# First attention of a two-block kernel: another order of head sums, low parts and exchanges

## The chip, the cores and the metric

The kernel runs on one core of one Trainium2 chip. The time is the device time of one execution in microseconds; the median of several executions is compared. The engines are TensorE (PE in the rows; PEld is its weight load), VectorE (DVE), ScalarE (ACT), GpSimd (POOL) and SyncE (SP). ACTq is ScalarE's queue where it issues DMAs.

## The reference, cut to what matters

Two models run one after the other on 256 tokens of width 1024: a recurrent layer, a feed-forward, an attention layer, a feed-forward, and then two layers of a second block. The change is in the attention layer:

```python
def attention_layer(x, norm_g, w_qkv, q_norm, k_norm, w_out):
    b, l, _ = x.shape
    h = rmsnorm(x, norm_g)
    qkv = (h @ w_qkv).reshape(b, l, 3, ATT_HEADS, ATT_HEAD_DIM)
    pos = jnp.arange(l, dtype=jnp.float32)
    q = partial_rope(rmsnorm(qkv[:, :, 0], q_norm), pos) * (ATT_HEAD_DIM ** -0.5)
    k = partial_rope(rmsnorm(qkv[:, :, 1], k_norm), pos)
    v = qkv[:, :, 2]
    ...
```

There are 16 heads of 64. `rmsnorm` of q and k is taken over each head. `partial_rope` turns the first 16 of the 64 features of a head: the first 8 and the next 8 change places and are multiplied with the sine, all is multiplied with the cosine, and the two are added.

## The kernel before

Activations lie feature-major, 8 tiles of 128 features by 256 tokens. Every weight matrix comes in units: 1024 x 128 for queries and keys, half of the depth by 256 columns for values. The layer has 8 query units (`att_q`), 8 key units (`att_k`) and 8 value units (`att_v[0]`, `att_v[1]`, 4 each); the texts call them q0 to q7, k0 to k7 and v0 to v7. Products of float32 are made of three passes: a weight unit is split into a high part in rounded form and a low part, the rest. ScalarE writes the high part (L722, `high_act(through)`: all units up to that one that are still due), VectorE subtracts to get the low part (L733, `split_v(through)`), and TensorE multiplies high by high, high by low and low by high, 24 matmuls in a unit (L708, and L697 for the values).

There are 5 slots for raw units and 3 for high parts. SyncE loads unit u (L638) when unit u-5 is used; ScalarE can write the high part of unit u when unit u-3 is used. Two units make a half product of 512 columns in one of two banks; VectorE takes it to `Q` or `K` with the token scale (L2466, `scaled_halves_v`), ScalarE takes the value halves (L3424, `head_tokens_act`). `scaled_halves_v` with `more` 2 first writes the low parts up to two units past the half it then takes.

The token scale of the layer's norm is made by ScalarE, is turned by two transposes on TensorE behind q7 (L949), and ScalarE reads the turned form (`RSTD`, L3443), which is only needed for the values.

For the norm of the heads VectorE squares `Q` (L2459, into `SQA`) and later `K` (into `SQK`); TensorE sums them over each head with four products (L941, `head_sums_pe`), ScalarE takes four logarithms (L3411) and one exponential (L3416, together `head_scales_act`), and VectorE multiplies (L2474, `norm_heads_v`). Then comes the rotation: ScalarE issues four DMAs that change the places of the first 8 and next 8 features of each head (L3434, `swap_halves_act`, SBUF to SBUF, into `ROT`, which a memset at L2497 has cleared), VectorE multiplies with the cosine (L2479, `cos_v`), multiplies `ROT` with the sine when the exchange has landed (L2485) and adds (L2488); these last two are `rotate_v`. After the rotation of `K` VectorE releases `keys_ready`, for which TensorE waits before the heads (L1201, `attend_pairs_pe`). Seven value units stand before that wait, v7 between the first scores of the heads.

Each engine's instructions stand in the order in which the functions write them by hand; an engine that waits holds up all that stands behind. Semaphores are counted, and `due` gives the count that the next event will have.

## Time and profile before

| | us |
|---|---|
| median of three runs | 1932.09 |
| lowest, highest | 1929.77, 1934.56 |
| profiled execution | 1930.44 |
| its span | 1927.4 |
| gap before k0, and start of the heads | 2.65, at 492.67 |

Times in the rows are microseconds from the start of the span; durations of one instruction in nanoseconds are marked. A name behind an arrow in brackets is what released the engine from the idle time given. Views used are the page (shares of the chain that ended last), the chain in order of time, the timeline of single engines, busy times in given stretches with the granted clock of TensorE, and the landing times of one tensor's transfers. TensorE's float32 products of 512 columns stand in the timeline as two matmuls each, so four head sums are counted as eight.

### The profile page before, as it was taken

To read this page: it belongs to the slowest core of one execution; us is meant where nothing else is said; L and a number is where in the kernel's file an instruction comes from. 1 tells how busy PE (TensorE), PEld (TensorE's weight loads), DVE (VectorE), ACT (ScalarE), POOL (GpSimd) and SP (SyncE) were. 2 spreads that over 40 slices of the span, in tenths; PEclk is the share of its full clock that TensorE was granted. 3 is DMA by queue.
4 is the path that set the end of the run, shared out by engine and by line. 5 is a ranking of instruction groups with operands and counts; after the bars stand their busy time and mean duration, and the time that the engine had idled before them with its cause. 6 is when DMAs were issued, how large, how long until landed. Compare 5 with 4: busy or idle time off the path is not lost.

```text
span 1927.4 us, 42678 instructions
## 1 busy us (share of the span) xinstructions
PE 1849.3 (96%) x18447; PEld 1728.3 (90%) x18447; DVE 1339.1 (69%) x1723; ACT 814.6 (42%) x1219; POOL 88.3 (5%) x131
## 2 busy tenths in 40 slices
PE   8999999999899999999998999998999999999999
PEld 7987999998689999998987799897998997889988
DVE  8897688757748876764786469666774696459755
ACT  5573534435634342223755234254213664235154
POOL 2000000000400000002000000000002000000000
PEclk9999999999999999999999999999999999999999
DMA  8555477974337795663550145554563651135644
GB/s 224 144 144 152 129 264 257 271 201 137 105 99 250 264 267 136 164 174 94 163 153 15 47 119 165 145 146 128 145 185 88 163 154 47 28 105 160 172 118 134
DMA packets 473228, 291.94 MB, mean 151 GB/s; under 512 B 26775, under 2 KB 467580, under 8 KB 472872
## 3 DMA queue, kind: packets, MB, share of 16 engines
q1 hardware_dynamic: 466720, 262.13, 48.5%
q0 software_dynamic: 5312, 25.32, 3.5%
q10 hardware_dynamic: 1032, 2.11, 0.5%
q8 instruction: 126, 2.06, 0.5%
q14 instruction: 38, 0.31, 0.1%
HBM read 287.95 MB, written 1.05 MB: 150 GB/s over the span
## 4 chain that ended last, share of the span: by engine, by line
PE 79%; DVE 14%; ACT 4%; issue 2%; DMA 1%; ACTq 0%; POOL 0%; DVEq 0%
PE bank L708 37%; PE bank L1486 6%; PE bank L1488 6%; PE bank L1487 6%; DVE rounded L733 4%; PE bank L667 3%; PE bank L949 3%; PE bank L697 2%; ACT rounded L722 1%; PE bank L1692 1%; PE bank L1679 1%; PE bank L1116 1%; DVE rounded L717 1%; PE bank L790 1%; PE bank L941 1%
## 5 line engine op out<-in xcount | busy, mean ns | idle before, releaser
L708 PE MATMUL bank<-rounded 128*128 128x256 f32 x5928 | 719.1, 281 | 10.2 <-DVE rounded L733 7.9
L708 PEld LDWEIGHTS bank<-rounded 128*128 128x128 f32 x5928 | 700.8, 187 | 25.2 <-DVE rounded L733 12.3
L733 DVE TENSOR_TENSOR rounded<-arena,rounded 128x1024 fp32r<-128x1024 f32 (+1 forms) x307 | 370.6, 1215 | 102.5 <-ACT rounded L722 94.6
L1486 PE MATMUL bank<-parts 128*128 128x256 f32 x1024 | 287.2, 280 | 1.0 <-DVE parts L2323 0.9
L1488 PE MATMUL bank<-parts 128*128 128x256 f32 x1024 | 285.9, 279 | 0.0
L1487 PE MATMUL bank<-parts 128*128 128x256 f32 x1024 | 285.6, 279 | 0.0
L722 ACT ACTIVATE rounded<-arena 128x1024 fp32r<-128x1024 f32 x192 | 201.5, 1057 | 170.2 <-PE bank L708 103.5
L1486 PEld LDWEIGHTS bank<-parts 128*128 128x128 f32 x1024 | 192.8, 188 | 2.2 <-issue 1.2
L1488 PEld LDWEIGHTS bank<-parts 128*128 128x128 f32 x1024 | 192.3, 188 | 0.0
L1487 PEld LDWEIGHTS bank<-parts 128*128 128x128 f32 x1024 | 192.1, 188 | 0.1
L773 ACT ACTIVATE arena<-bank 128x512 f32<-128x512 f32 x90 | 53.2, 596 | 241.6 <-PE bank L708 227.7
L2395 ACT ACTIVATE parts<-whole 128x2048 fp32r<-128x2048 f32 x44 | 84.3, 1918 | 126.9 <-PE bank L1488 109.4
L717 DVE CAST rounded<-arena 128x1024 fp32r<-128x1024 f32 (+1 forms) x115 | 78.2, 680 | 69.2 <-PE bank L708 43.0
L2315 DVE TENSOR_TENSOR parts<-whole,parts 128x2048 fp32r<-128x2048 f32 x44 | 100.7, 2292 | 16.8 <-ACT parts L2395 16.1
L708 PE MATMUL bank<-arena 128*128 128x256 f32 x416 | 91.1, 379 | 0.0
L949 PE MATMUL bank<-common,arena 128*128 128x128 f32 x519 | 78.1, 285 | 13.3 <-DMA common<-in_const 7.1
L708 PEld LDWEIGHTS bank<-arena 128*128 128x128 f32 x416 | 78.9, 190 | 11.5 <-issue 1.0
L708 PE MATMUL bank<-common,arena 128*128 128x256 f32 x384 | 87.8, 383 | 0.0
L708 PEld LDWEIGHTS bank<-common,arena 128*128 128x128 f32 x384 | 71.2, 189 | 10.9 <-issue 0.3
L949 PEld LDWEIGHTS bank<-common,arena 128*128 128x128 f32 x519 | 58.6, 145 | 23.0 <-DMA common<-in_const 7.1
L2323 DVE TENSOR_TENSOR parts<-whole,parts 128x1408 fp32r<-128x1408 f32 x32 | 52.0, 1625 | 38.9 <-ACT parts L2427 38.8
L2427 ACT ACTIVATE parts<-whole 128x1408 fp32r<-128x1408 f32 x32 | 44.1, 1380 | 65.9 <-PE bank L1488 54.5
(407 smaller groups left out, 2405.8 us busy)
## 6 DMA issues: line engine op xcount, KB each, us to landing
arena<-in_w_in SPq DMA_DIRECT2D x190, 512.0 KB, 3.8
whole<-in_ffn_w_gate_up SPq DMA_DIRECT2D x44, 1024.0 KB, 5.2
arena<-in_ada_w POOLq DMA_DIRECT2D x32, 768.0 KB, 6.4
whole<-in_ffn_w_down SPq DMA_DIRECT2D x16, 1408.0 KB, 7.2
arena<-in_rec_w_in SPq DMA_DIRECT2D x36, 512.0 KB, 3.8
arena<-in_att_w_qkv SPq DMA_DIRECT2D x24, 512.0 KB, 3.8
arena<-in_rec_w_out SPq DMA_DIRECT2D x16, 512.0 KB, 3.7
arena<-in_mla_w_o SPq DMA_DIRECT2D x16, 512.0 KB, 3.7
```

Source lines behind the costliest of these rows:

```text
L667: last = pe.matmul(psum[s][:, i * T:i * T + T], w[a][:, kk, :], job.rhs[b][:, kk, :], start=(i, kk, a, b) == (0, 0, 0, 0), stop=kk == job. ...
L708: last = pe.matmul(psum[s][0:c, m % 2 * T:m % 2 * T + T], w[a][:, k, cols], x[b][:, k, :], start=(k, a, b) == (0, 0, 0), stop=k == job.kt ...
L717: write(high_view(job_of[u], u), raw_view(job_of[u], u, UNIT_RAW)).then_inc(done.sem, 1)
L722: high_parts(act, lambda to, frm: act.activation(to, frm, ACT.Copy), high_by_act[0].pop(0), unit_high_s)
L733: dve.tensor_tensor(raw_view(job_of[u], u, UNIT_LOW), raw, high_view(job_of[u], u).bitcast(F32), ALU.subtract)\
L773: return lambda i, bank, done, rounds: act.activation(two(dst, i, lo), bank, func).then_inc(done, 1)
L949: last = pe.transpose(bank[:, n * P:n * P + P], x, ident)
L1486: pe.matmul(bank, w_hi, x_hi, start=start and k == 0, stop=False)
L1487: pe.matmul(bank, w_hi, x_lo, start=False, stop=False)
L1488: last = pe.matmul(bank, w_lo, x_hi, start=False, stop=stop and k == n - 1)
L2315: dve.tensor_tensor(UP_W[s][1], WHOLE_UP[s], UP_W[s][0].bitcast(F32), ALU.subtract)\
L2395: act.activation(UP_W[s][0], WHOLE_UP[s], ACT.Copy)\
```

## The change

TensorE sums the squares of the query heads behind k1 in place of k3, and those of the key heads behind v0 in place of v1. ScalarE writes the high parts of k0 and k1 before it reads the turned scale, no longer writes a high part between logarithms and exponential, and issues the exchange of Q behind one high part (k5's) after the exponential; before, the exchange stood behind those of k7, v0, v1 and v2, too. The exchange of K stands behind v5's high part as before; the second logarithms come ahead of v4's high part. VectorE clears `ROT` before the last query half, takes key halves one at a time between the steps of Q's rotation, and the rotation is cut in two functions, so that low parts and a key half stand between the sine multiply and the addition.

```diff
@@ att_pe
-            multiply_units(att_k, range(4))
+            multiply_units(att_k, range(2))
             head_sums_pe(SQA, DK, abanks)
-            multiply_units(att_k, range(4, 8))
-            multiply_units(att_v[0], range(2))
+            multiply_units(att_k, range(2, 8))
+            multiply_units(att_v[0], range(1))
             head_sums_pe(SQK, DK, abanks)
-            multiply_units(att_v[0], range(2, 4))
-            multiply_units(att_v[1], range(2))
-            multiply_units(att_v[1], range(2, 3))
+            multiply_units(att_v[0], range(1, 4))
+            multiply_units(att_v[1], range(3))
@@ attention_v
-            scaled_halves_v(att_q, Q, 2, range(4))
+            scaled_halves_v(att_q, Q, 2, range(3))
             dve.memset(flat(ROT), 0.0)\
                .then_inc(vector_step.sem, 1)
             dve.wait_ge(vector_step.sem, vector_step.due(dve))
+            scaled_halves_v(att_q, Q, 2, range(3, 4))
             square_heads_v(Q, SQA)
-            scaled_halves_v(att_k, K, 2, range(2))
-            split_v(att_k.first + 6)
+            scaled_halves_v(att_k, K, 2, range(1))
+            split_v(att_k.first + 4)
             norm_heads_v(Q, "att_q_norm")
-            scaled_halves_v(att_k, K, 2, range(2, 4))
+            scaled_halves_v(att_k, K, 2, range(1, 2))
+            cos_v(Q)
+            scaled_halves_v(att_k, K, 2, range(2, 3))
+            sin_v()
+            scaled_halves_v(att_k, K, 2, range(3, 4))
             square_heads_v(K, SQK)
-            cos_v(Q)
-            split_v(att_v[0].first + 2)
-            rotate_v(Q)
+            rotated_v(Q)
+            split_v(att_v[0].first + 3)
+            norm_heads_v(K, "att_k_norm")
             split_v(att_v[1].first)
-            norm_heads_v(K, "att_k_norm")
-            split_v(att_v[1].first + 1)
             cos_v(K)
+            split_v(att_v[1].first + 2)
+            sin_v()
             split_v(att_v[1].through())
-            rotate_v(K)
+            rotated_v(K)
@@ att_act
-            high_act(att_q.through())
+            high_act(att_k.first + 1)
...
-            high_act(att_k.first + 2)
+            high_act(att_k.first + 4)
+            head_scales_act()
             high_act(att_k.first + 5)
-            head_scales_act(att_k.first + 6)
-            high_act(att_v[0].first + 2)
             swap_halves_act(Q)
+            high_act(att_v[0].first + 3)
+            head_scales_act()
+            high_act(att_v[1].first)
             head_tokens_act(0, range(1))
-            high_act(att_v[1].first)
-            head_scales_act()
             high_act(att_v[1].first + 1)
             swap_halves_act(K)
+            high_act(att_v[1].first + 2)
             head_tokens_act(0, range(1, 2))
             high_act(att_v[1].through())
```

ScalarE in the order of before, from the reading of the turned scale to the exchange of K. L3443 is that reading, L722 a high part (x6: k0 to k5), L3411 the logarithms, L3416 the exponential, L3434 an exchange, L3424 a value half.

```order
L3443 ACTIVATE common<-bank 128x2
L722 ACTIVATE rounded<-arena 128x1024 x6
L3411 ACTIVATE arena<-bank,common 128x512 x4
L722 ACTIVATE rounded<-arena 128x1024
L3416 ACTIVATE arena<-arena 128x2048
L722 ACTIVATE rounded<-arena 128x1024 x4
L3434 DMA arena<-arena 8x2048 x4
L3424 ACTIVATE arena<-bank,common 128x256 x2
```

The same stretch in the changed kernel, where the lines are L3447, L3417, L3420, L3438 and L3428.

```order
L722 ACTIVATE rounded<-arena 128x1024 x7
L3447 ACTIVATE common<-bank 128x2
L722 ACTIVATE rounded<-arena 128x1024 x3
L3417 ACTIVATE arena<-bank,common 128x512 x4
L3420 ACTIVATE arena<-arena 128x2048
L722 ACTIVATE rounded<-arena 128x1024
L3438 DMA arena<-arena 8x2048 x4
L722 ACTIVATE rounded<-arena 128x1024 x6
```

Two of the high parts have moved ahead of the reading (x7: q3 to q7, k0, k1), and five that stood between the first logarithms and the first exchange are one.

VectorE in the order of before, from the norm of Q to its rotation. L2474 is the norm, L733 a low part, L2466 a key half taken, L2459 the squares of K, L2479 the cosine, L2485 the sine, L2488 the addition.

```order
L2474 SCALAR_TENSOR_TENSOR arena<-arena,common 128x2048
L733 TENSOR_TENSOR rounded<-arena,rounded 128x1024
L2466 TENSOR_TENSOR arena<-bank,common 128x512
L733 TENSOR_TENSOR rounded<-arena,rounded 128x1024 x2
L2466 TENSOR_TENSOR arena<-bank,common 128x512
L2459 TENSOR_TENSOR arena<-arena 128x2048
L2479 TENSOR_TENSOR arena<-arena,common 128x2048
L733 TENSOR_TENSOR rounded<-arena,rounded 128x1024
L2485 TENSOR_TENSOR arena<-arena,common 128x2048
L2488 TENSOR_TENSOR arena<-arena 128x2048
```

The same stretch in the changed kernel; its lines are L2473, L2465, L2458, L2478, L2484 and L2489.

```order
L2473 SCALAR_TENSOR_TENSOR arena<-arena,common 128x2048
L733 TENSOR_TENSOR rounded<-arena,rounded 128x1024
L2465 TENSOR_TENSOR arena<-bank,common 128x512
L2478 TENSOR_TENSOR arena<-arena,common 128x2048
L733 TENSOR_TENSOR rounded<-arena,rounded 128x1024 x2
L2465 TENSOR_TENSOR arena<-bank,common 128x512
L2484 TENSOR_TENSOR arena<-arena,common 128x2048
L733 TENSOR_TENSOR rounded<-arena,rounded 128x1024 x2
L2465 TENSOR_TENSOR arena<-bank,common 128x512
L2458 TENSOR_TENSOR arena<-arena 128x2048
L2489 TENSOR_TENSOR arena<-arena 128x2048
```

Cosine and sine of Q have moved ahead of the last key half and of the key squares, and with the sine the wait for the exchange.

## Rows read from the trace of the kernel before

**Rows 1.** The page: shares of the chain that ended last, by engine.

```profile
PE 79%; DVE 14%; ACT 4%; issue 2%; DMA 1%; ACTq 0%; POOL 0%; DVEq 0%
```

**Rows 2.** The chain in order of time, 430 to 505: start us, us, engine, line.

```profile
434.85 2.36 DVE rounded L733 x2
...
438.37 1.78 DVE arena L2497
...
449.70 3.43 PE bank L941 x8
453.13 11.32 PE bank L708 x96
...
466.72 5.05 DMA arena<-arena
...
478.73 2.35 DVE arena L2474
...
483.09 0.64 ACTq L3434
...
485.67 2.36 DVE rounded L733 x2
...
490.27 2.30 DVE arena L2488
```

**Rows 3.** Timeline of TensorE: start, us, line; idle time before it and its releaser.

```profile
436.18 7.18 PE L708 MATMUL bank<-parts,rounded 128*128 128x256 f32 x48 [2.65 <-issue]
443.78 5.92 PE L708 MATMUL bank<-parts,rounded 128*128 128x256 f32 x48 [0.42 <-DVE rounded L733]
...
473.49 1.13 PE L941 MATMUL bank<-arena,common 128*128 128x512 f32 x2 [0.82 <-ACT arena L3411]
...
477.73 8.43 PE L697 MATMUL bank<-rounded,parts 128*128 128x256 f32 x72 [0.37 <-DVE rounded L733]
486.95 2.99 PE L697 MATMUL bank<-rounded,parts 128*128 128x256 f32 x24 [0.79 <-DVE rounded L733]
492.67 0.93 PE L1201 MATMUL bank<-arena 64*128 64x128 f32 x8 [2.73 <-DVEq L2515]
...
494.33 1.22 PE L1201 MATMUL bank<-arena 64*128 64x128 f32 x6 [0.73 <-DVE arena L1245]
...
495.91 5.13 PE L697 MATMUL bank<-rounded,parts 128*128 128x256 f32 x24
```

**Rows 4.** Busy times in three stretches; the last three columns are PEclk, DMA share, GB/s.

```profile
435.80:439.00 3.20, 2.82 (x13) 2.85 (x14) 2.64 (x4) 0.91 (x1) 0.00 (x0) 0.50 0.21 64
472.00:474.00 2.00, 1.18 (x3) 0.30 (x2) 2.00 (x1) 1.97 (x3) 0.00 (x0) 1.00 0.80 266
493.80:500.60 6.80, 6.27 (x30) 5.65 (x31) 5.38 (x15) 3.29 (x12) 3.83 (x6) 0.51 0.02 4
```

**Rows 5.** Timeline of ScalarE, columns as in rows 3.

```profile
424.92 1.06 ACT L722 ACTIVATE rounded<-arena 128x1024 fp32r<-128x1024 f32 x1 [1.76 <-PE bank L708]
433.56 0.17 ACT L3443 ACTIVATE common<-bank 128x2 f32<-128x2 f32 x1 [7.58 <-PE bank L949]
...
454.92 1.90 ACT L3416 ACTIVATE arena<-arena 128x2048 f32<-128x2048 f32 x1
...
464.56 2.79 ACTq L3434 DMA_DIRECT2D arena<-arena  x4
...
501.13 0.84 ACT L3424 ACTIVATE arena<-bank,common 128x256 f32<-128x256 f32 x2 [2.02 <-PE bank L697]
```

**Rows 6.** Timeline of VectorE, columns as in rows 3.

```profile
464.47 0.69 DVE L2466 TENSOR_TENSOR arena<-bank,common 128x512 f32<-128x512 f32 x1 [0.45 <-PE bank L708]
```

**Rows 7.** Busy times at the end of K's exchange, columns as in rows 4.

```profile
485.00:485.50 0.50, 0.50 (x7) 0.50 (x6) 0.00 (x0) 0.50 (x2) 0.00 (x0) 1.00 0.14 33
485.50:486.00 0.50, 0.50 (x6) 0.46 (x5) 0.33 (x1) 0.50 (x2) 0.00 (x0) 1.00 0.01 0
```

**Rows 8.** Tile view of the loads of in_att_w_qkv.

```profile
DMA to landing us min/median/max: 3.4/3.8/10.3
```

More of the change, by code:

```diff
@@ L2481, in cos_v, with sin_v @@
             dve.wait_ge(vector_step.sem, vector_step.due(dve))
-        def rotate_v(x):
+        def sin_v():
             dve.wait_ge(heads_swapped.sem, heads_swapped.due(dve, 64))
@@ L2487, in rotate_v, with rotated_v @@
             dve.wait_ge(vector_step.sem, vector_step.due(dve))
+        def rotated_v(x):
             dve.tensor_tensor(x, SQA, ROT, ALU.add)\
@@ L3405, in modulation_act, with head_scales_act @@
             act.nop().then_inc(modulation_summed.sem, 1)
-        def head_scales_act(through=None):
+        def head_scales_act():
             for k in range(0, DK, 2):
@@ L3413, in head_scales_act @@
                 act.wait_ge(free.sem, free.due(act))
-            if through is not None:
-                high_act(through)
             act.activation(flat(RS), flat(RS), ACT.Exp, scale=-0.5)\
```

## The prediction

> **What bounds the kernel now.** I read the page's chain first, then the chain, TensorE's timeline, the clock and the other engines' rows between 415 and 505 us, since the change touches nothing else. TensorE carries 79% of the chain, VectorE 14% [rows 1]: the kernel is a sequence of products with a few places where another engine is late. The first attention is such a place. I call its weight units q0 to q7, k0 to k7 and v0 to v7; each is 24 matmuls. Four of them take 11.32 us in the chain, so one takes 2.83 us, and the four sums of a head-sum group take 3.43 us [rows 2]. TensorE finishes the q units and the two transposes of the scale at 433.53 and begins the heads at 492.67. In between lie 15 units and two sum groups: 15 x 2.83 + 2 x 3.43 = 49.3 us. Fifty-nine pass, so 9.8 us are lost. Where: 2.65 us before k0, 0.42 before k2, 0.82 inside the second sums, 0.37 and 0.79 before value units, 2.73 before the heads [rows 3], in sum 7.8. The rest is clock: after the first gap 435.8 to 439 ran at 0.50 of full clock, which is the 1.2 GHz level [rows 4], and 48 matmuls took 7.18 us in place of 5.66 [rows 3], 1.5 us more. Together 9.3, and 0.5 of pipeline edges.
>
> What releases them: ScalarE reads the turned scale at 433.56 and only then makes the high parts of k0 to k2 [rows 5], so the k0 low part starts at 434.85 [rows 2] with TensorE empty. At the far end the heads wait for the rotated keys. Their chain is norm 478.73, exchange issued until 483.73, two late low parts at 485.67, rotation to 492.57 [rows 2].
>
> **Durations** on VectorE: a low part 1.18 us (two in 2.36, [rows 2]), taking a half product 0.69 [rows 6], the multiplies over the whole of Q or K 2.30 [rows 2]. On ScalarE a high part takes 1.06 [rows 5].
>
> **Part 1, two high parts ahead of the turned scale.** A high part starts 0.38 us after the unit three before it is done: q7's starts at 424.92 [rows 5], when q4 ended at about 424.5 (three units before the transposes begin at 433.1). k0's and k1's can so be at 427.7 and 430.6, in time in which ScalarE waits 7.58 us for the transposes [rows 5]. Removed: their 2 x 1.06 us behind 433.56. VectorE meets them with the memset (1.78 us, [rows 2]) moved ahead of the low parts: last-but-one q product taken by 428.4, memset 428.9 to 430.7, low k0 to 431.95, low k1 from 431.7 + latency to 433.15. k0 starts at 433.53 as the transposes end. The 2.65 us gap and the 1.5 us of slow clock behind it go: 4.2 us. The cover is VectorE's idle time there; if it is gone, the price is again the same gap.
>
> **Part 2, first head sums behind k1.** The q product is taken at 433.3 (0.33 after q7's end), squares 434.1 to 436.5 (2.30 us, [rows 2]). k0 and k1 run to 439.2, so the squares are ready, and the sums fill 439.2 to 442.65. The last logarithm ends 4.2 us after a sum group starts (449.70 to 454.92, less one high part between them, [rows 2, 5]), the exponential takes 1.90 [rows 5]: 445.4. VectorE's norm (2.35 us, [rows 2]) ends at 447.8. What is queued behind the waiting norm on VectorE is low k5, which TensorE needs at 451.2 and gets at 449.0. ScalarE now has k5's high part behind the logarithms, 445.8 to 446.9.
>
> **Part 3, exchange at the norm.** ScalarE issues the four DMAs at 447.8 in place of 464.56, in 2.79 us [rows 5], until 450.6. They stand ahead of the high parts of k6 and k7, which come 450.65 to 452.75. VectorE: takes k's second half by 449.7, cos to 452.1, low k6 and k7 to 454.5; TensorE wants them at 454.0 for k6 (ready 453.3) and 456.8. The exchange before landed 5.05 us after its last issue began, with weight loads beside it [rows 2]: here 450.0 + 5.05 = 455.05. VectorE is busy until 455.3 anyway (it takes k's third half first), so the price now is nil; each later microsecond is one of delay, because the sine multiply now stands ahead of low v0 and v1, the last k half and the key squares. Sine 455.3 to 457.6, low v0 and v1 to 460.0, take to 460.7, squares 460.85 to 463.15. TensorE finishes k7 at 459.6 and v0 at 462.45, so it waits 0.7 us here, a gap of the kind at 473.49, whose 0.82 us left the clock at 1.00 [rows 3, 4]. Sums 463.2 to 466.65; before, they ended after 474.
>
> **Part 4, the keys.** Logarithms to 467.45, exponential to 469.4, key norm 469.4 to 471.8, while VectorE first adds the rotated Q and splits v2 and v3 (463.2 to 467.9). ScalarE must make v5's high part first, which needs v2 done (472.3): 472.7 to 473.75. Exchange issue 473.8 to 476.55, v6's high part to 477.6. VectorE: low v4 to 473.0, cos to 475.35, low v5, low v6 to 478.85. Landing is the unknown. The earlier row gives 5.05 us behind the start of the last issue. The second exchange of the kernel before had no weight load beside it: last issue at 483.09, last traffic at about 485.5, and none after [rows 2, 7], so 2.4 us. After the change the last weight load of the stage (v7's) is issued when v2 ends and takes 3.8 us [rows 8], to about 476.2, while the last exchange issue starts at 475.85. I take the row without load, since only the first 0.35 us of the last transfer lie beside it: 478.3, hidden behind low v6. Ends: 478.3 and 480.9. Then sine 478.9 to 481.2, low v7 to 482.4, rotation to 484.7, heads at 484.8. TensorE ends v6 at 483.6 and waits 1.2 us. **492.67 - 484.8 = 7.9 us gained** (5.8 with the late landing).
>
> A rule speaks against my choice here. The Trainium skill, "DMA: Bandwidth & Descriptors", section "Issuing engines are not separate DMA queues", says that transfers run on the same 16 DMA engines and interleave whichever engine issued them. By it ScalarE's exchange would share its time with SyncE's load of v7 and land late, a gain of 5.8 in place of 7.9; it is the third case below, and the trace agrees with it as far as 5.05 us with loads and 2.4 without go.
>
> **After the keys** the instructions are unchanged and take their waits with them. One thing can differ. Before, the gap of 2.73 us was followed by 0.51 of full clock from 493.8 to 500.6 [rows 4], and v7 took 5.13 us in place of 2.83 [rows 3], with ScalarE waiting 2.02 us for it [rows 5]. If the clock stays at 2.4 GHz, v7 and two small score products end 3 us earlier, and 2.0 of them are worth something until ScalarE's wait is used up. The total idle time there falls from 2.73 + 0.73 to about 1.2 + 0.73 us, which lies between gaps that cost the clock (2.65, 2.73) and one that did not (0.82); I give the fall two chances in three.
>
> **Sum.** The profiled execution took 1930.44 us, of which 1927.4 are its span; 1930.44 - 7.9 = 1922.5. It lay 1.65 us under the median of 1932.09, so the median comes to 1924.2, a gain of 0.41%. Nothing behind the stage has a time of its own: weight loads wait on used units, the feed-forward on the heads.
>
> **The cases.**
> - Forecast, 0.44: keys at 484.8, clock falls again: 1924.2.
> - Clock holds, 0.22: 7.9 + 2.0 = 9.9 us, 1922.2. For it: less idle. Against: two idle pieces close together.
> - Second exchange lands late, 0.16: 5.8 us, 1926.3. For it: 5.05 in the row of the first exchange; v7's load is issued 1.2 us before the exchange and runs beside it. Against: three of its four transfers are small and the load is nearly over.
> - Both exchanges late, 0.11: 2 us more on the first shift everything behind the sine of Q, 3.9 us, 1928.2.
> - The gain is given back, 0.03: the change makes keys earlier but the heads wait for something else, 1932.1. Against: the timeline shows nothing but the keys at 492.67 [rows 3].
> - Slower, 0.04: the first exchange blocks VectorE. Before, 4.6 us of issue and landing lay behind the key squares, now they are ahead of them, so lateness reaches TensorE. The longest landing of a load in the trace is 10.3 us [rows 8]. With 10.3 in both exchanges: the first shifts by 10.3 - 5.05 = 5.2, the key exchange lands at 475.85 + 5.2 + 10.3 = 491.4, plus 5.9 of sine, low part and rotation gives 497.3, 4.6 us behind before: 1936.7. It decides against the change once the two delays add to 7.9 us.
>
> **How the numbers follow.** A measurement here tells about 0.3%, 5.8 us, from no change. The first two cases lie beyond it, the third just at it (half counts): 0.74 faster. Half the third, the fourth and fifth: 0.22 same. 0.04 slower. The range must hold the clock case (1922.2), the two late exchanges (1928.2) and the spread of the three runs, 2.4 us to either side: 1920 to 1929.
>
> **What would show it.** Right: k0 right behind the transposes with the clock at 1.00 through 433 to 445; the four exchange issues of Q near 448 and of K near 474; waits of about 0.7 us before the second sums and 1.2 before the heads. Wrong: a DMA wait ahead of either sine multiply, a TensorE wait at k6 (its low part has 0.7 us to spare), or heads at 487 and later.

## The result and the profile after

| | before | changed |
|---|---|---|
| median, us | 1930.99 | 1919.67 |
| lowest, highest | 1929.77, 1934.56 | 1916.98, 1922.08 |
| profiled execution | 1930.44 | 1922.08 |
| its span | 1927.4 | 1920.3 |

The medians lie 11.3 us apart; the ratio of changed to before, estimated from all executions of the comparison, is 0.9943, 95% interval 0.9931 to 0.9956. (So estimated, a ratio need not be the quotient of the two medians, here and below.) The forecast was 1924.2, 7.9 us less, and the range began at 1920.0, so the time is 0.33 us outside it, on the better side.

The chain of the changed kernel in order of time, 430 to 505 us (start, us, engine, line), which answers to [rows 2]:

```profile
436.31 5.66 PE bank L708 x48
441.97 3.45 PE bank L941 x8
...
448.17 2.36 DVE arena L2473
450.55 0.83 ACTq L3438
...
452.76 5.90 DMA arena<-arena
...
458.79 2.30 DVE arena L2484
...
464.18 2.30 DVE arena L2458
466.52 3.70 PE bank L941 x8
...
477.98 4.31 DMA arena<-arena
482.32 2.30 DVE arena L2484
...
485.87 2.21 DVE arena L2489
...
488.18 0.93 PE bank L1201 x7
```

Read it from the top. k0 and k1 take 5.66 us (L708, 48 matmuls) and the first head sums (L941) follow without a gap. The exchange of Q is issued as the norm ends, and now it is in the chain: norm, issue, landing, sine, squares, second sums. The same three kinds come again for K. In [rows 1] DMA had 1% of the chain; in the page of the changed kernel it has 2%:

```profile
PE 78%; DVE 13%; ACT 4%; issue 2%; DMA 2%; POOL 0%; ACTq 0%; DVEq 0%; SPq 0%
```

TensorE's timeline of the changed kernel (start, us, line, count, and in brackets the idle time before it and what ended it), which answers to [rows 3]:

```profile
436.07 5.90 PE L708 MATMUL bank<-parts,rounded 128*128 128x256 f32 x48
...
444.84 17.52 PE L708 MATMUL bank<-parts,rounded 128*128 128x256 f32 x144
...
466.52 3.70 PE L941 MATMUL bank<-arena,common 128*128 128x512 f32 x8 [1.13 <-DVE arena L2458]
469.66 17.52 PE L697 MATMUL bank<-rounded,parts 128*128 128x256 f32 x144
488.18 0.93 PE L1201 MATMUL bank<-arena 64*128 64x128 f32 x8 [1.00 <-DVEq L2521]
...
490.70 3.00 PE L697 MATMUL bank<-rounded,parts 128*128 128x256 f32 x24
...
496.83 0.55 PE L949 MATMUL bank<-common,arena 128*128 128x128 f32 x3 [1.01 <-POOL arena L1284]
497.96 0.87 PE L1216 MATMUL bank<-arena 128*64 128x256 f32 x8 [0.58 <-ACTq L1304]
```

k0 has no bracket: the 2.65 us are gone. Two waits of a microsecond and more are left, 1.13 before the second sums and 1.00 before the heads. v7 takes 3.00 us where it took 5.13. The clock goes with the last; busy times in stretches of the changed kernel (length, busy us of PE, PEld, DVE, ACT and POOL, then granted clock, DMA share, GB/s), which answer to [rows 4]:

```profile
436.00:445.00 9.00, 9.00 (x60) 7.32 (x58) 7.26 (x6) 4.97 (x7) 0.00 (x0) 1.00 0.64 188
480.00:488.00 8.00, 7.18 (x61) 6.98 (x60) 6.85 (x5) 2.49 (x5) 0.00 (x0) 1.00 0.06 14
488.00:497.00 9.00, 6.91 (x56) 5.20 (x57) 6.89 (x19) 5.47 (x19) 4.49 (x6) 1.00 0.21 71
```

The third line is the stretch that stood at 0.51 in [rows 4]; here it is at 1.00, the 2.4 GHz level.

**A ruler for the stage.** The span is a poor ruler here: work ahead of the change, which is the same in all kernels below unless the text says otherwise, ends between 413.6 and 419.2 us in the profiled executions. So the stage is measured from the squares sum of the layer's norm that stands before q2 (L809, at 414.37 before and 417.16 changed), to the first score product ("keys", L1201) and from there to the first product with the values ("values", L1216):

| kernel | to keys | keys to values | sum |
|---|---|---|---|
| before | 78.30 | 11.76 | 90.06 |
| changed | 71.02 | 9.78 | 80.80 |
| changed, second profile | 70.26 | 9.77 | 80.03 |

The change brings 9.3 us (10.0 in the second profile) in its stage: 7.3 (8.0) up to the keys and 2.0 behind them. Two further profiles of the changed kernel come below; in one of them the part behind the keys is less.

### The profile page after: what moved, and what is told of

It is laid out like the page before. It is cut to its first block, busy times and chain, and to the rows that moved or that the text cites. A ratio compares the mean times of both kernels' runs of the same rounds, so it can differ in the third digit from the quotient of the medians.

```text
span 1920.3 us, 42684 instructions
## 1 busy us (share of the span) xinstructions
PE 1845.2 (96%) x18447; PEld 1725.7 (90%) x18447; DVE 1339.4 (70%) x1723; ACT 815.6 (42%) x1219; POOL 88.3 (5%) x131
## 4 chain that ended last, share of the span: by engine, by line
PE 78%; DVE 13%; ACT 4%; issue 2%; DMA 2%; POOL 0%; ACTq 0%; DVEq 0%; SPq 0%
PE bank L708 38%; PE bank L1486 6%; PE bank L1488 6%; PE bank L1487 6%; DVE rounded L733 3%; PE bank L949 3%; PE bank L667 3%; PE bank L697 2%; PE bank L1691 1%; ACT rounded L722 1%; PE bank L1678 1%; PE bank L1116 1%; PE bank L941 1%; DVE rounded L717 1%; PE bank L1659 1%
## 5 line engine op out<-in xcount | busy, mean ns | idle before, releaser
L708 PE MATMUL bank<-rounded 128*128 128x256 f32 x5928 | 721.2, 282 | 9.6 <-DVE rounded L733 7.3
L708 PEld LDWEIGHTS bank<-rounded 128*128 128x128 f32 x5928 | 703.0, 187 | 24.6 <-DVE rounded L733 11.9
L733 DVE TENSOR_TENSOR rounded<-arena,rounded 128x1024 fp32r<-128x1024 f32 (+1 forms) x307 | 370.7, 1215 | 90.0 <-ACT rounded L722 81.6
L722 ACT ACTIVATE rounded<-arena 128x1024 fp32r<-128x1024 f32 x192 | 201.9, 1057 | 182.4 <-PE bank L708 101.5
L708 PE MATMUL bank<-arena 128*128 128x256 f32 x416 | 91.1, 379 | 0.0
L708 PEld LDWEIGHTS bank<-arena 128*128 128x128 f32 x416 | 78.9, 190 | 11.5 <-issue 1.0
L708 PE MATMUL bank<-common,arena 128*128 128x256 f32 x384 | 87.8, 383 | 0.0
L708 PEld LDWEIGHTS bank<-common,arena 128*128 128x128 f32 x384 | 71.2, 189 | 10.9 <-issue 0.3
```

What stands on the lines that cost most here:

```text
L708: last = pe.matmul(psum[s][0:c, m % 2 * T:m % 2 * T + T], w[a][:, k, cols], x[b][:, k, :], start=(k, a, b) == (0, 0, 0), stop=k == job.kt ...
L722: high_parts(act, lambda to, frm: act.activation(to, frm, ACT.Copy), high_by_act[0].pop(0), unit_high_s)
L733: dve.tensor_tensor(raw_view(job_of[u], u, UNIT_LOW), raw, high_view(job_of[u], u).bitcast(F32), ALU.subtract)\
```

## The experiments

My theory, A: the gain is the three pieces of the walk, high parts ahead of the scale, earlier sums and exchanges, and the clock that holds behind the keys because the wait there is short. Rivals: B, one part alone brings it all; C, the 2 us behind the keys have another cause than the length of the wait; D, the exchanges are late because a load runs beside them; E, what is measured as more than 7.9 is the spread between executions. The expectations that are quoted below have letters of their own for their theories and rivals. Medians are given with that of the kernel before on the same chip, and the ratio with its 95% interval. The stage of a kernel is read from one profiled execution.

### The changed kernel again

No edit.

> The changed kernel once more, in more rounds. Theory A (keys earlier by 7.3 us, the clock at 2.4 GHz behind them worth 2.0, the rest of the 11 us spread between executions): 9.3 us under the kernel before, and in the trace v7 in about 3.0 us. Rival B (some further stage gained too, lastingly): 11 us or more again, and the trace shows where outside 430 to 500. Rival C (clock luck of one execution, it falls behind the keys in others): 7.3 us on average, v7 at about 5.1 us in some traces.

1917.45 beside 1928.86, ratio 0.9939 (0.9924 to 0.9954). The result repeats, and 11.4 us is the number of the rival in the quoted text and not of the theory. In its profile the span is 15.1 us under that of the kernel before, and only 10.0 of these lie in the stage: 1.6 lie between the first product with the values and the end of the heads (33.17 in place of 34.80) and 4.2 behind the heads. Whether those last, this run can't tell; the third and fourth comparison (below) gave 5.4 and 9.2 us, so that they don't always. The profiled execution had this in TensorE's timeline (columns as above):

```profile
419.63 13.88 PE L708 MATMUL bank<-parts,rounded 128*128 128x256 f32 x120 [0.68 <-DVE rounded L733]
```

The same 120 matmuls with the same 0.68 us ahead of them took 14.40 in the first profile. That has nothing to do with the change and is a part of the spread (last section).

### The high parts and the memset alone, on the kernel before

```diff
-            scaled_halves_v(att_q, Q, 2, range(4))
+            scaled_halves_v(att_q, Q, 2, range(3))
             dve.memset(flat(ROT), 0.0)\
...
+            scaled_halves_v(att_q, Q, 2, range(3, 4))
...
-            high_act(att_q.through())
+            high_act(att_k.first + 1)
```

> Part 1 alone on the kernel before: high parts of k0 and k1 ahead of the turned scale and the memset ahead of the last query half. My sum: 2.65 us of gap and 1.5 of slow clock go, all behind shifts, and the gap before the heads stays with its slow clock: 4.2 us under the kernel before. Rival (the gained time is waited out again at the first head sums or the keys): under 2 us.

1924.61 beside 1928.86, ratio 0.9970 (0.9956 to 0.9983). TensorE's timeline of this kernel:

```profile
433.97 11.55 PE L708 MATMUL bank<-parts,rounded 128*128 128x256 f32 x96
...
488.13 1.36 PE L1201 MATMUL bank<-arena 64*128 64x128 f32 x8 [2.73 <-DVEq L2516]
...
491.80 4.64 PE L697 MATMUL bank<-rounded,parts 128*128 128x256 f32 x24
```

k0 to k3 run through in 11.55 us, and the wait before the heads is the 2.73 us of [rows 3] again, with v7 again slow behind it. The stage is 5.3 us shorter. The walk said 4.2: it counted the 2.65 and the 1.5 of clock, but not the 0.42 before k2 and the 0.26 that k2 and k3 were over 5.66 in [rows 3], which go too. That makes 4.9; where the other 0.4 comes from isn't shown.

### The change without the high parts

The reverse of the last edit, on the changed kernel. The memset goes back behind the last query half, too.

> The changed kernel with part 1 undone. If the parts add, it keeps the difference: 9.3 - 4.2 = 5.1 us under the kernel before, with the gap of 2.65 us before k0 and the clock at 0.50 behind it back. Rival (the later start is absorbed by the waits of 1.1 us before the second sums and before the heads): 6 to 7 us under.

1931.53 beside 1928.86, ratio 1.0016 (0.9994 to 1.0039), so no gain at all, although the stage is 3.5 us shorter than before. The gap is back:

```profile
438.09 7.42 PE L708 MATMUL bank<-parts,rounded 128*128 128x256 f32 x48 [2.66 <-issue]
```

The executions fall in two groups. Six took 1923.8 to 1928.0 with granted clocks of 0.989 to 0.993 in the mean over the whole execution, and six took 1935.1 to 1942.3 with 0.982 to 0.986; the profiled one is of the second group. Its heads, in a stretch of 33 us:

```profile
504.00:537.00 33.00, 32.77 (x158) 24.24 (x158) 16.28 (x45) 15.65 (x51) 15.06 (x20) 0.50 0.39 102
```

About the same part of the heads in the second profile of the changed kernel:

```profile
494.00:527.00 33.00, 28.55 (x220) 21.39 (x221) 19.44 (x54) 22.10 (x67) 19.52 (x26) 1.00 0.46 127
```

TensorE is 99% busy, and runs at the 1.2 GHz level over the whole of it, with 158 matmuls where 220 fit. This was in no case of mine. I call it the long stretch. From the first product with the values to the end of the heads it took 46.38 us, where the kernel before and the first profile of the changed kernel took 34.80 and the second 33.17. An estimate from these rows: 33 us at half the clock lower the mean of a 1930 us execution by 0.009. So I take a mean at or below 0.986 as the mark of a long stretch in executions without a profile. The stretch itself was seen in two profiles, this one and one below.

### Only the high parts back, the memset where the change puts it

```diff
-            high_act(att_k.first + 1)
+            high_act(att_q.through())
```

> The changed kernel with only the two high parts put back behind the reading of the turned scale; the memset stays moved. By my sum the gap of 2.65 us before k0 and the slow clock behind it are back, 4.2 us, and the memset's place is worth nothing. If the clock in the heads' stage falls only by accident, 1922 in all executions; if it follows from the k0 gap, again two groups of executions, one at about 1925, one over 1937.

1923.78 beside 1929.77, ratio 0.9973 (0.9958 to 0.9989); in none of 12 executions was the clock at or below 0.986. So the long stretch doesn't follow from the gap before k0: with that gap it came in six of 12 executions of one kernel and in none of 12 of this one. The stage is 85.43, 4.6 over the first and 5.4 over the second profile of the changed kernel, and TensorE's timeline has the gap with the slow clock behind it:

```profile
435.60 7.42 PE L708 MATMUL bank<-parts,rounded 128*128 128x256 f32 x48 [2.73 <-issue]
```

Against the kernel without either (86.53), the memset's place is worth 1.1 us. Rival B falls: high parts and memset alone give 5.3 of the stage, the rest alone 3.5, in sum 8.8 of 9.3.

### A longer wait before the heads

```diff
             rotated_v(K)
+            dve.memset(flat(SQK), 0.0)\
+               .then_inc(vector_step.sem, 1)
+            dve.wait_ge(vector_step.sem, vector_step.due(dve))
             dve.nop().then_inc(keys_ready.sem, 1)
```

> The changed kernel with one more memset of 128x2048 (1.76 us) between the rotation of K and the release of the keys, so that the gap before the heads is 2.8 us, about what it was before. Theory A, the clock follows the length of that gap: it falls behind the keys, v7 takes about 5 us, and the kernel is 1.8 + 2.0 = 3.8 us over the changed one. Rival C, the clock has nothing to do with the gap: 1.8 us over.

1923.86 beside 1928.86, ratio 0.9969 (0.9956 to 0.9981), 6.4 us over the changed kernel of the same comparison. TensorE's timeline:

```profile
470.18 16.90 PE L697 MATMUL bank<-rounded,parts 128*128 128x256 f32 x144
490.45 0.93 PE L1201 MATMUL bank<-arena 64*128 64x128 f32 x8 [3.38 <-DVEq L2524]
...
493.69 3.92 PE L697 MATMUL bank<-rounded,parts 128*128 128x256 f32 x24
```

The wait is 3.38 us and v7 takes 3.92: with the wait the clock loss is back, and "keys to values" goes from 9.77 to 10.56. The sign is as A says and the size is not: the clock part was to cost 2.0 us and costs 0.8. The total is more than the stage shows (3.3), and the other 3 us stay unexplained beside the spread between executions.

### Neither high parts nor a short wait

Both edits, the reverse of the high parts and the memset before the keys. If the long stretch comes from a clock that was not brought down ahead of the heads, it must vanish here.

> Part 1 undone, and one memset of 1.76 us more before the keys are released. Without part 1, 6 of 12 executions had a granted clock of 0.986 or less and were over 1935 us. Theory T (the slow clock inside the heads' stage hangs on where the short waits behind the keys fall, and a long gap before the keys, which brings the clock down early and lets it recover under v7, avoids it): no execution under 0.988, median about 3 us over the fast half of that kernel (1926), 1929. Rival (it comes from the gap before k0): again about half of the executions over 1937.

1930.44 beside 1929.77, ratio 0.9998 (0.9982 to 1.0013). None of 12 executions lies at or below 0.986, where six of 12 did without the longer wait. In the profile the wait before the heads is 3.12 us and v7 takes 5.23. The stage is 89.91. So the kernel whose stage is 3.4 us longer comes out no worse against the kernel before. This was the first sign that a clock that falls for v7 alone (2 us) can spare one that falls in the heads (12 to 16 us by the medians of the groups).

### The last load held back until the exchange has landed

```diff
+                if job is att_v[1] and i == 3:
+                    sp.wait_ge(heads_swapped.sem, 128)
...
             sin_v()
-            split_v(att_v[1].through())
             rotated_v(K)
             dve.nop().then_inc(keys_ready.sem, 1)
+            split_v(att_v[1].through())
```

> The changed kernel with SyncE's load of v7 held until the exchange of K has landed, and the low part of v7 behind the release of the keys. Theory L (the weight load beside it makes the exchange late): the last transfer lands 2.4 us behind the start of its last issue in place of 4.3, the sine no longer waits 1.1 us for it, and with the low part moved the keys come about 2.3 us earlier; v7 then arrives later, which may cost about 1 us behind the keys. Rival (the landing of four small transfers takes over 4 us in any case): the sine still waits about 1.1 us, the keys come only 1.2 us earlier.

1919.56 beside 1929.77, ratio 0.9958 (0.9938 to 0.9979), one of 12 with the low clock (1934.65). SyncE's queue, ScalarE's queue and VectorE in this kernel's timeline:

```profile
469.32 8.76 SPq L640 DMA_DIRECT2D arena<-in_att_w_qkv  x2
...
472.13 2.62 ACTq L3440 DMA_DIRECT2D arena<-arena  x4
...
477.67 2.29 DVE L2486 TENSOR_TENSOR arena<-arena,common 128x2048 f32<-128x2048 f32 x1
```

The four issues end at 474.75, the last starts near 474.1, VectorE starts the sine at 477.67, and SyncE, which waits for the landing, issues v7's load at 477.71: the exchange takes 3.5 us with v7's load not beside it. In four profiles of the changed kernel, with it, it took 4.31, 4.18, 4.02 and 4.22. VectorE starts the sine without a wait that the timeline shows, and the wait before the heads is gone. The stage is 79.05, 1.0 to 1.8 under the changed kernel. D holds for 0.5 to 0.8 us, and the landing without load is still not the 2.4 us that I read from the traffic.

### Exchange and second sums sooner

```diff
@@ attention_v
             scaled_halves_v(att_k, K, 2, range(2, 3))
+            split_v(att_v[0].first)
             sin_v()
@@ att_act
             head_tokens_act(0, range(1))
-            high_act(att_v[1].first + 1)
             swap_halves_act(K)
```

> The changed kernel with the exchange of K issued ahead of v5's high part (0.65 us earlier) and the low part of v0 ahead of the sine of Q, in the 1.0 us that VectorE waits for the exchange. Theory A (both waits for the exchange are on the path): second sums 0.6 us earlier, keys 1.0 to 1.3 us earlier, so about 1 us under the changed kernel, 1917. Rival (landing shifts with the load beside it, not with the issue): the first 0.6 only.

1923.01 beside 1929.77, ratio 0.9968 (0.9948 to 0.9988): no better than the change, and not the 1 us better that I expected. In the timeline the wait before the second sums fell to 0.55, and in the chain the landing of K's exchange rose from 4.31 to 5.38:

```profile
465.51 3.70 PE L941 MATMUL bank<-arena,common 128*128 128x512 f32 x8 [0.55 <-DVE arena L2458]
...
487.61 0.99 PE L1201 MATMUL bank<-arena 64*128 64x128 f32 x8 [2.07 <-DVEq L2522]
```

```profile
476.35 5.38 DMA arena<-arena
```

Counted from the start of the stage, K's exchange was issued 1.4 us sooner and landed 0.3 sooner, with more of the load beside it. The wait before the heads became 2.07, the clock fell, and v7 took 5.01 us. "To keys" is 70.69, "keys to values" 11.74.

### Both together, and the sooner exchange with the wait filled

Two kernels. The first has the edits of the last two kernels together. The second is the last kernel (exchange and second sums sooner, load not held) with 14 matmuls ahead of the wait for the keys whose products nobody reads; its edit, beside that of the last kernel, is:

```diff
             multiply_units(att_v[1], range(3))
+            for _ in range(14):
+                pe.matmul(psum[4][:, 0:T], H_PARTS[0][:, 0, 0:P], H_PARTS[0][:, 1, :], start=True, stop=True)
             pe.wait_ge(keys_ready.sem, keys_ready.due(pe))
```

> The changed kernel with three more edits: the exchange of K ahead of v5's high part, the low part of v0 ahead of the sine of Q, SyncE's load of v7 held until the exchange of K has landed (low part of v7 behind the release of the keys). With the load held alone TensorE had no gap before the heads. Theory A (TensorE is then the bound from the second sums on): second sums and keys 0.6 us earlier than with the load held alone, 1.6 earlier than in the changed kernel, clock at 2.4 GHz behind the keys, about 1.5 to 2 us under the changed kernel. Rival (the exchange does not land sooner for being issued sooner): a gap of 1 us or more stays before the heads and the median is that of the changed kernel or above.

> The kernel with the sooner exchange of K and the earlier low part of v0 (its median was 1923.0, with a gap of 2.07 us before the heads and v7 at 5.0 us), now with 14 unread matmuls (1.65 us) in that gap. Theory A: the clock holds, v7 3.0 us, 2.0 us under that kernel in the stage and fewer slow executions, 1918 to 1920. Rival (that kernel is slower for another reason): 1923 again.

Both together: 1919.87 beside 1927.45, ratio 0.9977 (0.9950 to 1.0003). The stage is the shortest of all, 78.32, and yet four of 12 executions took 1933.1 to 1935.8 at clocks of 0.981 to 0.986. The profiled one is one of them (L1218 is L1216 of the other kernels, two added lines further down):

```profile
500.13 1.55 PE L1218 MATMUL bank<-arena 128*64 128x256 f32 x8
...
506.92 1.55 PE L1218 MATMUL bank<-arena 128*64 128x256 f32 x8
```

```profile
494.00:534.00 40.00, 39.09 (x183) 28.11 (x181) 17.83 (x50) 18.80 (x59) 18.54 (x25) 0.50 0.35 91
```

The products with the values of two pairs of heads stand 6.79 us apart; at the full clock they stand 4.0 apart.

The second kernel, with the wait filled: 1918.32, ratio 0.9962 (0.9941 to 0.9983), v7 back at 3.00 us, one of 12 at the low clock (1934.21). Its stage is 80.48, 2.0 under the same kernel with the idle wait. The ratios of the two, 0.9962 and 0.9968, do not tell them apart, so this is a reading of the profiles. The same wait for the keys, once idle and once with TensorE at work, goes with a slow and with a fast v7, here and in the next experiment. So the idleness of TensorE there matters, and rival C falls so far. That its length alone decides is not shown (see the fourth profile of the changed kernel below).

### The kernel before with the wait filled

The same edit with 20 matmuls, on the kernel before.

> The kernel before with 20 matmuls that nothing reads (128x256, into a bank that is free) before TensorE's wait for the keys, 2.4 of the 2.73 us of that gap. The keys come when they came. Theory A (the idle time brings the clock down and that costs 2.0 us under v7): v7 takes 3.0 us in place of 5.1, first value products 9.8 us behind the keys in place of 11.8, 2.0 us under the kernel before. Rival (the slow stretch behind the keys comes from the small score products, not from the gap): no change.

1934.04 beside 1927.45, ratio 1.0038 (1.0009 to 1.0067). In its timeline:

```profile
494.18 2.54 PE L1572 MATMUL bank<-parts 128*128 128x256 f32 x20
497.07 0.93 PE L1201 MATMUL bank<-arena 64*128 64x128 f32 x8 [0.35 <-DVEq L2517]
...
499.59 3.09 PE L697 MATMUL bank<-rounded,parts 128*128 128x256 f32 x24
```

v7 takes 3.09 and the stage is 2.4 us shorter, as A says, but five of 12 executions took 1941.7 to 1945.0. The clock held for v7 is paid back there, and more. The long stretch is not all of it: the seven other executions average 1929.4, where those of the kernel before average 1927.7, and the profiled one, which is among the seven, has a short slow stretch in the heads, its first two products with the values 5.52 us apart in place of 4.0. The rest is open.

### The changed kernel twice more

No edit. The first stood beside the last three kernels, the second beside the three of the next section.

> The changed kernel beside the three others, for their comparison on one chip and for the number of executions in which the clock of the heads' stage stays down (none of 10 so far). Theory A: 9.3 to 10 us under the kernel before plus at most 1.5 of other clock luck, 1918 to 1920; if the excess over the stage was chance, the ratio comes back to 0.995.

> The changed kernel beside the others. Over the three comparisons so far 22 executions, one of them slow by its clock. Theory G: 8 to 10 us under the kernel before on average, one execution in 10 or 20 over 1933.

1922.04 beside 1927.45, ratio 0.9971 (0.9950 to 0.9992), one of 12 at the low clock (1935.54). 1921.68 beside 1930.84, ratio 0.9957 (0.9938 to 0.9976), two of 12 (1932.16 and 1933.06). So by the mean clock the changed kernel has the long stretch too, in 3 of 34 executions.

The two profiles are of other executions, and each shows the clock fall where the first two did not:

| kernel | to keys | keys to values | sum |
|---|---|---|---|
| changed, third profile | 70.70 | 9.77 | 80.47 |
| changed, fourth profile | 70.39 | 10.42 | 80.81 |

In the third it falls behind the first product with the values; the next stands 5.96 us later in place of 4.0:

```profile
499.22 0.87 PE L1216 MATMUL bank<-arena 128*64 128x256 f32 x8 [0.58 <-ACTq L1304]
...
505.18 1.55 PE L1216 MATMUL bank<-arena 128*64 128x256 f32 x8
```

In the fourth it falls behind the wait for the keys, which is 1.33 us, and v7 takes 3.79; two microseconds of that stretch follow as busy times and clock:

```profile
485.87 0.93 PE L1201 MATMUL bank<-arena 64*128 64x128 f32 x8 [1.33 <-DVEq L2521]
...
489.11 3.79 PE L697 MATMUL bank<-rounded,parts 128*128 128x256 f32 x24
```

```profile
488.00:490.00 2.00, 2.00 (x12) 1.35 (x10) 1.83 (x6) 1.48 (x6) 0.09 (x1) 0.50 0.00 0
```

The kernel with only the high parts back waited 1.32 us there, and its v7 took 3.01. So the length of the wait alone doesn't decide, and the 2.0 us behind the keys are 1.3 in one of four profiles of the changed kernel.

### The two short waits at the start of the heads filled

Theory: the clock is lost in the heads when TensorE comes at full clock to the two waits at their start, 1.01 and 0.58 us in the timeline of the changed kernel. The edit puts 7 and 4 matmuls there whose products nobody reads, on the changed kernel, on "both together", and on the kernel before with its filled wait.

```diff
+            def unread(n):
+                s = att_out.at % 2
+                pe.wait_ge(taken[s].sem, att_v[1].at // 2 + 1)
+                for _ in range(n):
+                    pe.matmul(psum[s][:, 0:T], H_PARTS[0][:, 0, 0:P], H_PARTS[0][:, 1, :], start=True, stop=True)
             for p in range(DK):
+                if p == 1:
+                    unread(7)
                 turn_probs_pe(2 * p)
                 if p == 1:
+                    unread(4)
```

> The changed kernel with 7 and 4 unread matmuls (128x256, free bank) in the two waits of 1.01 and 0.59 us between v7 and the first value products. Theory G (these waits bring the clock down at the start of the heads, and it then stays down in some executions, 13 to 15 us): no execution with a mean clock of 0.986 or less, the rest as the changed kernel, so 9.5 to 11 us under the kernel before and a smaller spread. Rival (the small products themselves keep the clock down, the waits have no part in it): slow executions as often as beside it, and no gain.

> The kernel with exchange, v0's low part and v7's load changed (4 of its 12 executions were over 1933 us at 0.981 to 0.986) with the same two fillings. Theory G: no execution over 1925, median about 1917. Rival: about a third of the executions over 1933 again.

> The kernel before with 20 unread matmuls in the gap before the keys and 7 and 4 in the two waits at the start of the heads. With the 20 alone, 5 of 12 executions were over 1941 us and the median 6 us above the kernel before. Theory G: the slow executions go and the 2.0 us under v7 stay, 2 us under the kernel before. Rival: again two groups.

On the changed kernel 1918.65 beside 1930.84, ratio 0.9941 (0.9928 to 0.9953). On "both together" 1918.91, ratio 0.9945 (0.9932 to 0.9958). On the kernel before with its filled wait 1932.38, ratio 1.0011 (1.0002 to 1.0020), where 2 us under the kernel before were expected. In the first of them TensorE's timeline has

```profile
492.90 1.07 PE L1227 MATMUL bank<-parts 128*128 128x256 f32 x7
494.15 0.55 PE L949 MATMUL bank<-common,arena 128*128 128x128 f32 x3 [0.18 <-POOL arena L1293]
...
495.28 0.87 PE L1216 MATMUL bank<-arena 128*64 128x256 f32 x8
```

and the second, in the 40 us that stood at 0.50 without the filling,

```profile
494.00:534.00 40.00, 36.12 (x252) 28.33 (x249) 24.57 (x56) 24.18 (x65) 18.02 (x24) 1.00 0.50 135
```

Counted over all executions whose clock is on record, those with a mean granted clock at or below 0.986. A kernel is put into a line by v7 in its profiles:

| | kernels | at or below 0.986 |
|---|---|---|
| clock already down for v7 | before; high parts alone; longer wait; neither; sooner | 1 of 161 |
| clock at full level for v7 | changed; without high parts; only high parts back; held load; both together; before filled; sooner filled | 20 of 106 |
| the same, waits at the heads filled | the last three kernels | 0 of 22 |

The third line against the second speaks for the theory (at 20 in 106 each, 22 executions without one have a chance of 1 in 100); "both together" alone went from 4 of 12 to 0 of 5. The grouping was made after most of the runs, inside the second line the kernels differ from 0 of 12 to 6 of 12, and the fourth profile of the changed kernel, with v7 at 3.79, fits neither of the first two lines. The comparison that needs no grouping is that of one kernel with and without the edit: the kernel before with its filled wait went from five of 12 to 0 of 12 (a chance of 2 in 100 if the edit did nothing), though in another comparison and on another chip. And the mark counts long stretches only. Shorter ones, which cost 1.5 to 3 us in the heads, are in profiles of kernels of the second line (held load, before filled, changed), and one is left near 530 us in the profile of the kernel before with both fillings. And the kernel before with both fillings takes 1.5 us more than without, though its stage is 2.1 us shorter (87.98) and no execution has the mark of the long stretch. Its profile places such a loss outside the edited part: 2.5 us more ahead of the stage, 2.1 less in it, the same in the heads, and 3.1 more behind them. In that profile the clock is down near 150 and 1070 us, where it was full in the profile before; but over its 12 executions the mean clock is 0.992, not under the 0.991 of the kernel before, so this doesn't explain the median. Why the same instructions take longer there stays open, as does why the long stretch comes in 6 of 12 executions of one kernel and in 3 of 34 of another.

The changed kernel with filled waits has the lowest median of the last comparison (0.9941 beside 0.9957 of the changed kernel in the same comparison; medians 1918.65 and 1921.68). The intervals overlap, so that it beats the change is likely and not settled.

## Why the prediction was nearly right and its range was not

All times of this section are on the scale of the profile before, that is, those of the changed kernel's first profile less the 2.79 us by which its stage began later.

**Part 1.** Forecast 4.2 us; alone it brings 5.3, taken back it costs 4.6 to 5.4. The cover, VectorE idle ahead of the transposes, held. k0 starts at 433.3 (forecast 433.53). The term was too small by 0.7 us: the wait before k2, which I had listed among the losses and not counted, and the slowness of k2 and k3. Another 0.4 is not placed.

**Part 2.** Exchange of Q issued at 447.76 (forecast 447.8). Sums, logarithms, exponential and norm came as laid out.

**Part 3.** The exchange landed 5.90 us behind the start of its last issue, not 5.05, and VectorE waited 1.01 us for it where I had it arrive as VectorE came free. "Each later microsecond is one of delay" was right: the wait before the second sums is 1.13 in place of 0.7, and the sums begin at 463.73 (463.2).

**Part 4, the step that was mis-sized.** I took 2.4 us for the landing of K's exchange, from the end of its traffic in [rows 7]. It took 4.31, and VectorE waited 1.12 us. The experiment with the load held shows both halves of the mistake: 3.5 us even without v7's load, since the end of traffic is not the landing, and 0.5 to 0.8 more with it. Nor did only 0.35 us of the last transfer lie beside the load: v7's load was issued 0.1 us before the exchange (475.91 and 476.00 on the profile's own scale) and not 1.2, so it lay beside more of it. (The prediction also calls three of the four small; the trace has all four at 64 KB.) The third case, the late landing, had its mechanism right and 0.16 for a chance; the rule of the Trainium skill ("DMA: Bandwidth & Descriptors", "Issuing engines are not separate DMA queues") that I weighed and set aside fits: 3.5 us without v7's load, 4.31 with it, and 5.38 with more of it beside. What the lateness cost was small, since VectorE was late itself: keys at 485.4 against 484.8, 7.3 us of gain against 7.9.

**After the keys, the step that failed.** I gave the clock 0.44 to fall and 0.22 to hold. It held in three of four profiles, worth 2.0 us, the size that I had worked out, and fell in part in the fourth, worth 1.3. My reason for the fall was the sum of two idle pieces close together. At this point waits of 2.07, 2.73, 3.12 and 3.38 us were followed by a v7 of 5.01, 4.64 to 5.13, 5.23 and 3.92 us, those of 0.32 to 1.32 us by one of 3.00 to 3.09, and one of 1.33 us by one of 3.79. So the row of 0.82 at [rows 3] was the nearer one for a wait of 1.00, but the clock also depends on something that the length of the wait doesn't give.

**The range.** 7.3 + 2.0 = 9.3 us from 1930.99 or 1932.09 gives 1921.7 or 1922.8, inside the range. So the failed step moved the forecast, and what put the result outside the range is its last term, the 2.4 us for the spread of three executions. (Nor are the edges what the prediction says: 1922.2 - 2.4 is 1919.8, and 1928.2 + 2.4 is 1930.6, not 1929.) That 1919.67 fell below both is luck of four executions. The rest to 1919.67 is spread between executions (E): the four comparisons of the changed kernel gave differences of the medians of 11.3, 11.4, 5.4 and 9.2 us, and the differences of the means, weighted with its 34 executions, come to 8.3 us. I had taken the spread from three executions of the kernel before. The profiles show three things that differ between executions of one kernel: the two rates of the matmuls (last section); the long stretch, which is in no case of the prediction and takes back some 1 us of the 9.3 to 10.0 on average (3 of 34, 12 to 16 us each, an estimate); and short stretches at the 1.2 GHz level far from the changed stage, as here, 150 us into the second and the third profile of the changed kernel:

```profile
150.00:155.00 5.00, 4.76 (x19) 3.71 (x20) 4.50 (x12) 1.49 (x2) 0.00 (x0) 1.00 0.00 0
```

```profile
150.00:155.00 5.00, 3.21 (x7) 1.77 (x7) 4.61 (x9) 1.49 (x2) 0.00 (x0) 0.71 0.00 0
```

Added up over the span, TensorE stood at that level for some 34 us in the profile before and for 27, 17, 31 and 27 in the four of the changed kernel. The mean granted clock of the changed kernel's executions was 0.994 in the comparisons that gave 11.3 and 11.4 us, and 0.991 and 0.992 in those that gave 5.4 and 9.2. The sentence "nothing behind the stage has a time of its own" put this at zero; from the first product with the values to the end of the heads alone the profiles go from 33 to 49 us.

## What to carry to other kernels

A landing is the instruction that waits for it, not the end of the traffic; take a transfer's time from a row that ends in a release, and add the loads that will then run beside it. A wait shortened on TensorE can be worth its length plus what the matmuls behind it lose at half clock, but look also at what comes after: work with short waits in it, entered at the full clock, lost the clock here for longer than the wait was, in some executions. Judge a change of this size by its stage in several traces, and by more than a dozen executions: two comparisons with 12 of the changed kernel gave 5.4 and 9.2 us.

## What the runs showed of the hardware that I had not expected

**A busy TensorE can stay at 1.2 GHz.** In stretches of 33 and 40 us TensorE was 99 and 98% busy at a granted clock of 0.50, in the heads' scores, transposes and products with the values, which take 1.55 us in place of 0.87. By the mean clocks it does not happen in all executions of one program.

**Two rates at one clock.** With the granted clock at 1.00 the same matmuls of 256 columns come at two rates: v1 to v6, 144 matmuls, took 17.52 us in the changed kernel and 16.90 with the longer wait (and 16.91 in the fourth profile of the changed kernel), and the 120 of q3 to q7 took 14.40 and 13.88. The ratio is 1.037 in both. Which of the two applies changes between executions and between stretches of one.
